# A hybrid encoder step: decays of the delta branch clipped by Relu, two masks of GpSimd dropped and one moved, filler spread otherwise

## The reference

```python
G = jnp.cumsum(gb, axis=-1)
decay = jnp.exp(jnp.where(tri, G[..., :, None] - G[..., None, :], -jnp.inf))
a = jnp.where(strict, jnp.einsum('bhik,bhjk->bhij', kb, kb) * decay, 0.0) * bb[..., :, None]
lower = eye + a
u = lax.linalg.triangular_solve(lower, vb * bb[..., None], ...)
...
o = (jnp.einsum('bhck,bhkv->bhcv', qb * jnp.exp(G)[..., None], s)
     + jnp.einsum('bhij,bhjv->bhiv', jnp.einsum('bhik,bhjk->bhij', qb, kb) * decay, u))
```

## Time and profile before

| what | value |
|---|---|
| median of 3 runs | 3297.74 us (3291.78 to 3300.55) |
| the profiled execution | 3301.59 us, span 3299.80 us |
| mean granted TensorE clock | 0.969 of 2.4 GHz |
| TensorE busy | 3029.9 us, 92% |
| VectorE, ScalarE, GpSimd busy | 35%, 30%, 26% |

### The profile page before, as it was taken

The page is one execution under the profiler, slowest core; times in us unless marked ns, Lnnn a source line. Parts: engine busy times, 40 slices in busy tenths (PEclk is TensorE's granted clock), DMA queues, the critical chain, the costliest instruction groups (busy, mean ns, idle before and its releaser), DMA issues. The chain is left out here.

```text
span 3299.8 us, 55375 instructions
## 1 busy us (share of the span) xinstructions
PE 3029.9 (92%) x23900; PEld 2716.9 (82%) x23900; DVE 1169.1 (35%) x2533; ACT 995.4 (30%) x1754; POOL 844.0 (26%) x536
## 2 busy tenths in 40 slices
PE   5899999999898898999989999999998898899996
PEld 2887888888798887999857888888887887899995
DVE  2412142333534533155142112342335525522632
ACT  3221333223434534321040214233224434432201
POOL 0121212212423423332112112212213323324320
PEclk9899999999999999999989999999999999999998
DMA  7212112212111111243432202212211211123424
GB/s 262 72 41 90 66 57 91 80 41 85 49 52 53 57 45 54 88 172 102 150 139 84 92 28 93 68 59 86 84 43 48 57 51 47 57 70 136 137 94 168
DMA packets 109890, 275.98 MB, mean 84 GB/s; under 512 B 38288, under 2 KB 44560, under 8 KB 108496
## 3 DMA queue, kind: packets, MB, share of 16 engines
q1 hardware_dynamic: 109648, 272.45, 24.3%
HBM read 214.81 MB, written 62.05 MB: 84 GB/s over the span
## 5 line engine op out<-in xcount | busy, mean ns | idle before, releaser
L250 PE MATMUL ps<-sb_h_split,sb_w_split 128*128 128x364 f32 (+1 forms) x3312 | 1174.9, 355 | 62.7 <-PEq L223 30.2
L251 PE MATMUL ps<-sb_h_split,sb_w_split 128*128 128x364 f32 (+1 forms) x3312 | 1097.4, 331 | 0.9 <-issue 0.9
L252 PE MATMUL ps<-sb_h_split,sb_w_split 128*128 128x364 f32 (+1 forms) x3312 | 1096.4, 331 | 0.0
L250 PEld LDWEIGHTS ps<-sb_h_split,sb_w_split 128*128 128x128 f32 x3312 | 632.3, 191 | 130.2 <-issue 84.8
L304 POOL CAST sb_w_split<-sb_w_raw 128x1024 fp32r<-128x1024 f32 x154 | 169.1, 1098 | 1990.5 <-PE ps L252 1649.9
L251 PEld LDWEIGHTS ps<-sb_h_split,sb_w_split 128*128 128x128 f32 x3312 | 633.6, 191 | 9.5 <-issue 4.0
L252 PEld LDWEIGHTS ps<-sb_h_split,sb_w_split 128*128 128x128 f32 x3312 | 630.9, 190 | 0.0
L306 POOL TENSOR_TENSOR sb_w_split<-sb_w_raw,sb_w_split 128x1024 fp32r<-128x1024 f32 x154 | 374.6, 2433 | 12.3
L1193 DVE COPY sb_fox<-ps 128x512 f32<-128x512 f32 (+3 forms) x208 | 107.1, 540 | 325.7 <-PE ps L1086 325.7
L292 ACT ACTIVATE sb_raw_qk<-ps 128x364 f32<-128x364 f32 (+2 forms) x176 | 64.5, 393 | 333.2 <-PE ps L252 333.2
L1657 DVE SCALAR_TENSOR_TENSOR sb_delta<-sb_raw_qk,sb_delta_small,sb_delta 128x1024 f32<-128x1024 f32 x96 | 146.7, 1574 | 13.4 <-ACT sb_delta L1505 12.3
(11 more groups left out here) (264 smaller groups left out, 4527.1 us busy)
## 6 DMA issues: line engine op xcount, KB each, us to landing
sb_w_raw<-in_wblk SPq DMA_DIRECT2D x154, 512.0 KB, 5.2
sb_raw_qk<-scratch_gate SPq DMA_DIRECT2D x24, 544.0 KB, 3.6
sb_fox<-scratch_fcum SPq DMA_DIRECT2D x8, 1600.0 KB, 7.1
sb_w_raw<-in_wbr SPq DMA_DIRECT2D x48, 256.0 KB, 4.1
sb_w_raw<-in_adaw SPq DMA_DIRECT2D x20, 512.0 KB, 15.9
sb_norm_layer<-scratch_x SPq DMA_DIRECT2D x8, 1088.0 KB, 9.2
scratch_gate<-sb_fox SPq DMA_DIRECT2D x16, 544.0 KB
scratch_gate<-sb_delta SPq DMA_DIRECT2D x16, 544.0 KB
```

The costliest lines, as they stand in the source:

```text
L250: pe.matmul(out, w_hi, x_hi, start=first, stop=False)
L251: pe.matmul(out, w_hi, x_lo, start=False, stop=False)
L252: return pe.matmul(out, w_lo, x_hi, start=False, stop=last)
```

## The change

In the delta group the exponent is made by ScalarE: nine Relu, one for each chunk of 128 frames, compute relu(gcol - Grow), and the exponential takes it with scale -1. For pairs in the right order that is what was there; in the wrong order the exponent is zero where it was -1e30, and the factor one. GpSimd's subtraction and its two masks ahead of the exponential go. `brow * E` is no longer strictly triangular (the level masks and the blocks that are read see to that), and `E` for the k q products is masked with a 0/1 matrix `upper` behind the exponential, on GpSimd; VectorE waits for that mask only ahead of L1689. The exponential of E waits for the Relus, and no longer for GpSimd. The constant masks shrink from 8 to 7 planes.

The filler of the delta group has four turns less in the front and four more in the chain's steps. In the fox group one turn stands between any two banks of transposes of a tile, and three turns instead of five behind the last.

```diff
-            fill_probs = [5] * 9
+            fill_turns = [2 * ((len(blocks_of(t)) + 3) // 4) - 1 for t in range(9)]
+            fill_probs = [3] * 9
...
                                 mm.then_inc(bank_ready, 1)
+                                if (h, c // 4) != (1, (len(blk) - 1) // 4):
+                                    turns(fill, 1)
                         turns(fill, fill_probs[t])
...
-            front_turns = [24, 5, 12, 3, 4]
+            front_turns = [24, 4, 10, 2, 4]
...
-            step_turns = [5] * 6 + [6] * 3
+            step_turns = [5] * 2 + [6] * 7
...
                     pool.wait_ge(params_loaded, 80)
-
-                    pool.tensor_tensor(Q4(E), Q4(Grow), gcol.unsqueeze(2).to_broadcast([P, NTILE, P]),
-                                       ALU.subtract).then_inc(beta_decay, 1)
                     pool.tensor_tensor(kdc.unsqueeze(2), Q4(Grow)[:, :, P - 1:P], gcol.unsqueeze(2),
-                                       ALU.subtract)
-                    pool.wait_ge(beta_decay, 1)
-                    pool.tensor_tensor(Q4(E), Q4(E), tiles_of(future), ALU.subtract).then_inc(decays, 1)
-                    pool.tensor_tensor(Q4(brow), Q4(brow), tiles_of(strict), ALU.mult).then_inc(beta_decay, 1)
+                                       ALU.subtract).then_inc(decays, 1)
                     pool.wait_ge(proj_done, 3)
                     split_block(pool, L, first + 2)
                     pool.wait_ge(exps, 1)
-                    pool.wait_ge(beta_decay, 2)
                     pool.tensor_tensor(brow, brow, E, ALU.mult).then_inc(beta_decay, 1)
+                    pool.tensor_tensor(Q4(E), Q4(E), tiles_of(upper), ALU.mult).then_inc(beta_decay, 1)
...
                     take_into(act, 1, 1, B0, NB, ub[2])
+                    act.wait_ge(params_loaded, 80)
+                    for t in range(NTILE):
+                        ins = act.activation(Q4(E)[:, t, :], Q4(Grow)[:, t, :], ACT.Relu, bias=gcol[:, t:t + 1],
+                                             scale=-1.0)
+                    ins.then_inc(act_step, 1)
                     silu(0, 2)
...
                     kept(0)
+                    act.wait_ge(act_step, 1)
+                    act.activation(E, E, ACT.Exp, scale=-1.0).then_inc(exps, 1)
+                    act.activation(rt[0][:, 0:TOK], rt[0][:, 0:TOK], ACT.Exp, scale=-0.5).then_inc(inverse, 1)
                     act.wait_ge(decays, 1)
-                    act.activation(E, E, ACT.Exp).then_inc(exps, 1)
-                    act.activation(rt[0][:, 0:TOK], rt[0][:, 0:TOK], ACT.Exp, scale=-0.5).then_inc(inverse, 1)
                     act.activation(kdc, kdc, ACT.Exp).then_inc(exps, 1)
...
-                    dve.wait_ge(beta_decay, 3)
+                    dve.wait_ge(beta_decay, 1)
...
+                    dve.wait_ge(beta_decay, 2)
                     for n, (t, c) in enumerate(G3):
                         dve.wait_ge(bank_ready, 10 + n)
                         dve.tensor_tensor(Q4(AT)[:, t:t + c, :], Q4(ps[:, ring.bank(9 + n), 0:P * c]),
```

More of the change, by code:

```diff
@@ L58, in shape_constants @@
     ident = np.eye(P)
-    future = np.where(i[:, None] > i[None, :], 1e30, 0.0)
-    strict = (i[:, None] < i[None, :]).astype(float)
+    upper = (i[:, None] <= i[None, :]).astype(float)
     lev = []
@@ L70, in shape_constants @@
     small = np.concatenate([small, np.zeros((P, 2, 32))], axis=1).reshape(P, 2, P)
-    masks = np.concatenate([np.stack([ident, np.ones((P, P)), future, strict, causal, swap], axis=1), small], axis=1)
+    masks = np.concatenate([np.stack([ident, np.ones((P, P)), upper, causal, swap], axis=1), small], axis=1)
     half = 32
@@ L137, in build @@
         raw_qk = sb("raw_qk", [P, 2, UW])
-        masks = sb("masks", [P, 8, P])
+        masks = sb("masks", [P, 7, P])
         dsmall = sb("delta_small", [P, 8 * 21 + DEPTH])
@@ L144, in build @@
         modT = sb("modT", [P, 24, 2])
-        ident, ones, future, strict = (masks[:, m, :] for m in range(4))
-        causal, swap = masks[:, 4, :], masks[:, 5, :]
-        small = masks[:, 6:8, :].rearrange("p a c -> p (a c)").rearrange("p (m c) -> p m c", c=B)
+        ident, ones, upper, causal, swap = (masks[:, m, :] for m in range(5))
+        small = masks[:, 5:7, :].rearrange("p a c -> p (a c)").rearrange("p (m c) -> p m c", c=B)
         eps_c, l2_c, one_c = consts[:, 0:1], consts[:, 1:2], consts[:, 2:3]
@@ L994, in fox_group @@
             fill_scores = [0] + [2] * 8
-            fill_probs = [5] * 9
+            fill_turns = [2 * ((len(blocks_of(t)) + 3) // 4) - 1 for t in range(9)]
+            fill_probs = [3] * 9
             fill_out = [5] * 8 + [0]
             def filled(t):
-                return fill_start + sum(fill_scores[:t + 1]) + sum(fill_probs[:t + 1]) + sum(fill_out[:t])
+                return (fill_start + sum(fill_scores[:t + 1]) + sum(fill_turns[:t + 1]) + sum(fill_probs[:t + 1])
+                        + sum(fill_out[:t]))
             with nc.Block() as block:
@@ L1584, in _ @@
                     act.wait_ge(exps, 2)
-                    act.wait_ge(params_loaded, 80)
                     for n in range(3):
```

## The result

| | before | after |
|---|---|---|
| median | 3299.14 us | 3207.56 us (3206.55 to 3208.62) |
| ratio, 95% interval | | 0.9719 [0.9707, 0.9731] |
| the profiled execution, its span | 3301.59, 3299.80 us | 3208.62, 3206.2 us |
| mean granted clock | 0.969 | 0.985 |

The kernel is 2.8% faster. (One of the four executions of before, three times as long as the others, is left out of the ratio; the median of the other three is 3297.74 us.) The two spans lie 93.6 us apart; forecast were 82.

The account below looks back on a forecast made before the run. TensorE, busy 92% of the span, was taken as the bound, so only its waits and slow clock counted. Delta groups 57 us plus fox groups 25 us made 82 us, giving a median of 3216 us, range 3190 to 3260.

Parts of the forecast that it names:

- step 1: Delta group, VectorE: without GpSimd's subtraction and two masks the q convolution takes 4.51 us, ending at 987.35, not 996.8.
- The rival that GpSimd isn't what holds it: Delta group: the q convolution stays late though GpSimd's work goes; 3277 us, chance 0.06.
- step 2: Delta group, ScalarE: nine Relus take 2.43 us without table loads; squares of q end at 990.25.
- that rival: Delta group, ScalarE: Relu brings two table loads of 1.28 us, 20.5 us back, 3237 us; chance 0.12.
- steps 3 and 4: Delta front, TensorE: 7.51 us squares wait goes; waits become 2.1 (first Ln), 0.35 (k norm), 1.05 us (q norm).
- step 5: Delta group: new GpSimd mask ends at 1006.6, holds VectorE's SBUF-only copies 0 to 0.9 us, middle taken; L1677 unheld.
- step 6: Delta front: TensorE waits 1.9 us for the last transpose bank; level products start at 1012.3, before at 1022.21.
- step 8: Delta front: low clock after the new waits costs about 1.5 us; half charged, 0.75 us a group.
- the clock stays low: Rival: four short waits keep the delta groups' clock at 0.50 through the levels; 3366 us, chance 0.04.
- fox term: Fox groups: 26.4 us of copy waits go, 1.2 us charged for less cover of the last copies; net 25 us.
- more than forecast: Rival: shorter Relus, no hold of the copies, no low clock; 15 us more, 3201 us; chance 0.13.
- Step 7: Delta group: levels 9.9 us earlier, of which four turns, 2.0 us, only moved at the same price; gain 7.9 us.

Follow-up runs that it names:

- e2: The kernel before, with GpSimd's decays started only after VectorE's q convolution, all work and turns kept: 3269.32 us, ratio 0.9908.
- e5: The changed kernel with one needless full-width GpSimd product ahead of its nine columns, beside the q convolution: 3243.2 us, ratio 0.9832.
- e7: The changed kernel without the 0/1 mask behind the exponential and VectorE's wait for it: 3207.16 us, ratio 0.9726.
- e3: The changed kernel with the delta groups' filler turns as in the kernel before: 3195.2 us, ratio 0.9688.
- e4: The changed kernel with nine filler turns more in the delta front and seven less in the steps: 3206.51 us, ratio 0.9717.
- e8: The changed kernel with a needless full-width GpSimd product beside the q convolution, and GpSimd's split waiting for that convolution's end: 3220.65 us, ratio 0.9758.

## Why the prediction was right, and which terms were mis-sized

- **What holds the convolution (step 1): shown.** The 64-column instructions are back at 277 ns, and e2 frees the q convolution by moving GpSimd's work alone. The rival that GpSimd isn't what holds it is out, from both sides (e2 and e5). The split did miss the convolution, but by 0.03 us, and that is luck: step 1 let it overlap by some tenths and priced that at nothing, where e5 shows what an overlap costs: beside the split's first operation a 64-column instruction takes 1.09 us for 0.28.
- **Relu (step 2).** 2.73 us for 2.43, no table load; that rival is out. The squares of q end 13.5 us after the first tap, forecast 13.4.
- **The new waits (steps 3 and 4).** The forecast counts a wait from the moment at which TensorE could have started the next matmul, the rows from the modelled end of the last one, which is later. Counted as in the forecast: first Ln 1.9 us for 2.1 (1.76 in the row), k norm 0.32 for 0.35 (0.16), q norm 0.86 for 1.05 (0.70). The q norm ends 27.22 us after the first tap; the forecast says 27.2.
- **The mask and the copies (step 5): half of a term too much.** The forecast let the mask hold the diagonal copies for 0.45 us, the middle of its bounds. It holds them not at all: 1.82 us for four as without it. e7 confirms that the mask costs nothing. The rest of the step holds: the mask ends 29.7 us after the tap (forecast 29.8), since it makes no headway before the q norm ends, and L1678, from PSUM, is not held beside it: 1.73 us for three, the 2 us each named as a sign of being wrong did not come.
- **The transpose bank (step 6): mis-sized, 1.1 us for 1.9 (0.91 in the row).** The bank is free 0.55 us sooner than forecast, 0.45 of it the copies, and TensorE arrives 0.3 us later. So the level products start 35.10 and not 35.5 us after the tap: 0.4 us a group, 3 us.
- **A wait not counted.** The kernel before had a wait of 0.38 us for ScalarE's evacuation of a segment of filler in each delta group, some 100 us after the first tap (eight, 3.0 us). It is not in TensorE's list after, and with the old turns (e3) it is back: the other spread of the turns removed it.
- **The clock (step 8): the largest miss.** 0.75 us a group were charged, 6 us in all, by analogy to a group start that was followed by 3.4 us at 0.50. None of the eight fronts shows a stretch below 1.00, with waits of 0.2 to 1.8 us in each. The rival "the clock stays low" is out. That there was no low clock at all is seen in one execution each of after and e7; e4 and e8 have 3.4 us of it or more behind waits of 1.6 and 2.2 us in some groups and not in others, so the charge was not baseless, only not due here.
- **Sum.** 7.9 - 0.75 = 7.15 us a group were forecast. With 0.4 (levels), 0.4 (the wait not counted) and 0.75 (clock) it is 8.7, for 8.6 measured. The terms are the second group's and the groups gain between 6.4 and 10.6 us, so that it closes within 0.1 us is partly luck. The fox term, 25 us, is 24.5; the fear of a thin cover cost 1.3 us (L1097) where 1.2 were set down. The time, 3207.6, lies between the forecast's centre and the rival "more than forecast"; of that rival's three terms two came true, no hold of the copies and no low clock, and shorter Relus did not.
- **What the forecast priced at nothing and was not.** Step 7 lets the four turns that leave the front be "only moved". They were indeed done at the same price, but in the front they had covered waits that the change itself left open. e3 puts them back and gains 12 us. The redistribution is a loss inside the change; the sums of steps 3 and 4 had it (each wait is as long as the turns are few), but never asked what the old numbers of turns would give.

## What to carry to other kernels

Look at an instruction's smallest shape beside another engine's work: a 64-column operation that takes nine times its own time is held, and the remedy here was to take work off the other engine at that moment; work that was only moved (e2) held the next instructions with two SBUF inputs. When a long wait goes, read what the shorter ones behind it can hide and put filler there first, but follow each finished segment of filler to the engine that must empty its bank. And read margins: here two engines' work lay 0.03 us apart, and a needless operation of 2.5 us that made them meet cost 23 us by the meeting and 13 by itself.

## What the runs showed of the hardware that was not expected

- **The hold by form.** Beside GpSimd's full-width operations VectorE's instructions with two SBUF inputs are held: 277 to 2391 ns for 64 columns. Those with one PSUM and one SBUF input are not (L1678, 1.73 us for three beside the full-width L1345, and the same in e7 with nothing beside them), nor were copies of 32x288 from SBUF to SBUF (444 ns each, beside L1345 or beside nothing). The Trainium skill, GPSIMD Engine Reference, section 1, counts Vector instructions in a 2-port mode as contending as well; no run shows which mode these copies are in. They take 444 ns, and L1685, with two inputs and as many columns, 459: they are no faster for having one input only.
- **The hold works both ways.** GpSimd's L1345 takes 3.70 us where L1344, of the same shape, takes 2.64; L1344 in the earlier trace rows shows the same 3.63 beside 2.63. In both places it starts while a VectorE instruction with two SBUF inputs still runs, and ends 2.5 us after that one's end: after, VectorE's q norm ends at 982.57 + 2.84 = 985.41 and L1345 at 984.22 + 3.70 = 987.92; before, VectorE's instruction ends at 989.92 and L1344 at 988.81 + 3.63 = 992.44. The two engines take turns: the q norm itself ends only 1.15 us after L1344 has (984.26), with 1.29 us to do alone. That GpSimd waits in its turn is read from these times, not from a run that isolates it.
- **No length of wait decides alone on the low clock.** In the delta fronts of after waits of TensorE up to 1.8 us were never followed by 0.50. One of 3.4 us (e5) was, for 6.8 us in every group; one of 7.5 us (before) for 13.65 us in seven groups, and one of 5.97 us for 10.24 us in the eighth. e2, with 5.2 us, had 6.83 us in six groups and 3.41 in two. But e8, with 2.2 us behind 0.4 to 1.0 us, had 3.4 or 6.8 us in five groups and none in three, and e4 had 3.4 us in five groups around the levels, where its waits are 1.5 to 1.7 us. The same list of instructions thus met it in some groups and not in others.
